# Two experts per token chosen tile by tile, with three of the choices inside later norms

## What is computed

```
u = rmsnorm(x) * (1 + sc1) + sh1
m = mixer(u)                       # input projection, RG-LRU group and retention group, output projection
x = x + g1 * rmsnorm(m)
u2 = rmsnorm(x) * (1 + sc2) + sh2
p_group = softmax(u2 @ w_rg + b_rg)                # 4 groups
g_sel = argmax(p_group)
e_logits = u2 @ w_re + b_re                        # 16 experts, 4 a group
top_w, top_i = top_k(softmax(e_logits of g_sel), 2)
f = sum of the two experts (256 wide, silu-gated), weighted by p_g * top_w / sum(top_w)
x = x + g2 * rmsnorm(f)
```

## Time and profile before

| | us |
|---|---|
| median of three runs | 573.47 (573.0 to 574.8) |
| the profiled execution, its own time | 574.29 |
| its span in the profile | 572.3 |
| TensorE busy | 550.2 (96% of the span) |
| DVE busy | 212.0 (37%) |
| ScalarE busy | 166.4 (29%) |
| POOL busy | 98.5 (17%) |
| mean granted clock of TensorE | 0.991 |

### The profile page before, as it was taken

One profiled execution on the slowest core, in us unless ns is written; L12 is line 12 of the kernel. 1 busy time (PEld: TensorE's weight loads), 2 busy tenths in 40 slices (PEclk: granted clock), 3 DMA queues, 4 the chain that ended last, 5 costly groups with the idle time before them and its releaser, 6 DMA issues.

```text
span 572.3 us, 6747 instructions
## 1 busy us (share of the span) xinstructions
PE 550.2 (96%) x2562; PEld 341.4 (60%) x2562; DVE 212.0 (37%) x526; ACT 166.4 (29%) x326; POOL 98.5 (17%) x116
## 2 busy tenths in 40 slices
PE   7899999999999999999999999799999999999984
PEld 6577755544454555574444455677777777777641
DVE  3434386421232233325433656422223223221137
ACT  7332676712123122322323343111112112111142
POOL 3016000133000000003100211313232422232110
PEclk8999999999999999999999999999999999999998
DMA  8999997899300000089400359969999999999564
GB/s 278 356 332 338 333 351 318 296 389 340 133 1 0 0 1 1 1 286 350 118 37 37 111 177 314 274 229 340 338 326 344 354 349 332 331 354 344 125 203 166
DMA packets 73492, 133.15 MB, mean 233 GB/s; under 512 B 4138, under 2 KB 49618, under 8 KB 71410
## 3 DMA queue, kind: packets, MB, share of 16 engines
q1 hardware_dynamic: 58864, 99.36, 50.3%
q0 software_dynamic: 9536, 28.75, 18.1%
q10 hardware_dynamic: 5058, 4.58, 2.4%
HBM read 117.47 MB, written 18.35 MB: 237 GB/s over the span
## 4 chain that ended last, share of the span: by engine, by line
PE 87%; DVE 5%; DMA 4%; ACT 2%; issue 1%; ACTq 0%; SPq 0%
PE psum L717 82%; PE psum L720 4%; DMA ring<-in_w_mod_dram 2%; DMA out_dram<-arena 1%; DVE arena L2203 1%; ACT arena L1365 1%; DVE x L2207 1%; DMA hy<-in_c_sample_dram 1%; DVE arena L2044 0%; ACT L1365 0%; DVE arena L2125 0%; DVE arena L2258 0%; ACT ss L1365 0%; ACTq L1605 0%; ACT hy L1365 0%
## 5 line engine op out<-in xcount | busy, mean ns | idle before, releaser
L717 PE MATMUL psum<-ring,arena 128*128 128x256 f32 (+1 forms) x640 | 173.5, 427 | 1.8 <-DVE arena L2258 1.3
L717 PEld LDWEIGHTS psum<-ring,arena 128*128 128x128 f32 x640 | 120.3, 192 | 38.8 <-issue 25.8
L717 PE MATMUL psum<-ring,uT 128*128 128x512 f32 (+1 forms) x384 | 126.5, 522 | 0.0
L1365 ACT ACTIVATE arena<-psum 128x512 f32<-128x512 f32 (+6 forms) x111 | 50.7, 478 | 229.8 <-PE psum L717 202.8
L717 PEld LDWEIGHTS psum<-ring,uT 128*128 128x128 f32 (+1 forms) x384 | 56.5, 172 | 60.1 <-issue 55.8
L717 PE MATMUL psum<-uT,ring 128*128 128x288 f32 x256 | 64.9, 410 | 1.3 <-ACT uT L1365 1.3
L717 PEld LDWEIGHTS psum<-uT,ring 128*128 128x128 f32 x256 | 47.7, 190 | 17.5 <-issue 5.1
L720 PEld LDWEIGHTS psum<-con,arena 128*128 128x128 f32 (+1 forms) x295 | 35.5, 145 | 21.4 <-issue 14.1
L720 PE MATMUL psum<-con,arena 128*128 128x128 f32 (+1 forms) x295 | 42.2, 280 | 4.1 <-DVE arena L2303 3.1
L2303 DVE TENSOR_TENSOR arena<-arena,psum 128x256 f32<-128x256 f32 x16 | 6.7, 421 | 98.5 <-ACT arena L1365 98.5
L1365 ACT ACT_TABLE_LOAD x33 | 42.3, 1283 | 3.1 <-issue 2.1
(11 more groups left out here) (214 smaller groups left out, 421.8 us busy)
## 6 DMA issues: line engine op xcount, KB each, us to landing
ring<-in_w_mod_dram SPq DMA_DIRECT2D x24, 1024.0 KB, 11.4
ring<-in_w_exp_gate_dram SPq DMA_DIRECT2D x16, 1024.0 KB, 10.9
ring<-in_w_exp_up_dram SPq DMA_DIRECT2D x16, 1024.0 KB, 16.6
ring<-in_w_exp_down_dram SPq DMA_DIRECT2D x16, 1024.0 KB, 11.7
ring<-in_w_in_dram SPq DMA_DIRECT2D x10, 1024.0 KB, 14.3
ring<-in_w_out_dram SPq DMA_DIRECT2D x4, 1024.0 KB, 14.9
f_dram<-in_consts_dram POOLq DMA_DIRECT2D x1, 3072.0 KB, 20.5
arena<-in_state_ret_dram POOLq DMA_DIRECT2D x6, 512.0 KB, 5.4
```

What stands on the lines that cost most here:

```text
L717: return nc.tensor.matmul(out, lhsT, rhs, start=first, stop=last)
L1365: return nc.scalar.activation(out, src, func, **kw).then_inc(done, 1)
```

## The change

Each tile's choice is made alone, by `first_choice(t)` and `second_choice(t)`, with per-partition scalars where the version before had broadcast tensors. Tile 0's is put into `after_mixer(2)`, tile 1's into `after_mixer(3)`, the first part of tile 2's into `after_mixer(4)`, all between the count of `s_x1` and the wait for the root; the second part of tile 2's comes behind `after_mixer(4)`, and those of tiles 3 and 4 behind their `take_logits`. `s_rsel` now counts tiles. The difference of logits for the gates and one comparison for all tiles follow behind the last choice. On TensorE, the sum of tile 3's logits comes ahead of tile 4's transposes, with two fillers ahead of it; the second half of `state_step(1)` moves behind the rank sums, `add_state(1)` behind the first `slot_tokens`, and the four fillers ahead of the wait for `sel` go. The buffers of the choice lie elsewhere in the same arena.

```diff
--- before.py
+++ after.py
@@ -267,8 +267,8 @@
         gx = rtb[:, 0:25].rearrange("p (t g) -> p t g", g=5)
         rtop, rtmp, rm1, rm2 = (rtb[:, 25 + 5 * i:30 + 5 * i] for i in range(4))
         rgrp = rtb[:, 48:68].rearrange("p (t g) -> p t g", g=NG)
-        lem = region(14336 + 2 * TILES * NE, TILES, NE)
-        oh = [region(14336 + i * TILES * NE, TILES, NE) for i in range(2)]
+        lem = region(12800 + 2 * TILES * NE, TILES, NE)
+        oh = [region(12800 + i * TILES * NE, TILES, NE) for i in range(2)]
         rank1 = region(14336 + 3 * TILES * NE, TILES, NE)
         gsl = [region(14784 + i * NE, NE) for i in range(2)]
         spare = region(14816, 1)
@@ -1174,19 +1174,19 @@
             pair_sum(1)
             state_step(0, (1,))
             route_parts(3)
+            keep_running(2, 1)
+            route_sum(3)
             turn_u2(4)
-            route_sum(3)
             keep_running(3, 1)
             route_parts(4)
             keep_running(1, 1)
             route_sum(4)
             add_state(0)
-            state_step(1)
+            state_step(1, (0,))
 
 
             pe.wait_ge(s_u2Te, 2 * TILES)
-            keep_running(4, 4)
-            pe.wait_ge(s_rsel, 1)
+            pe.wait_ge(s_rsel, TILES)
             pe.wait_ge(s_clear, 6)
             pe.wait_ge(s_x1, TILES)
             pe.wait_ge(s_lg, TILES)
@@ -1200,7 +1200,7 @@
                 last = mm(bank[7][:, TILES * NE:(TILES + 1) * NE], ones[0:n], sel[0:n, j], j == 0,
                           j == TILES - 1)
             last.then_inc(s_rank, 1)
-            add_state(1)
+            state_step(1, (1,))
 
             def slot_tokens(e):
 
@@ -1213,6 +1213,7 @@
                 last.then_inc(s_tokn, 1)
 
             slot_tokens(0)
+            add_state(1)
 
             with pe.If(fits(pe)):
                 def turn_input(e):
@@ -2058,6 +2059,42 @@
 
             tag = lambda t: "p" if t < TILES - 1 else "s"
 
+            def first_choice(t):
+
+                dve.wait_ge(s_lg, t + 1)
+                lg, le, one = logit[:, t, 0:NG], logit[:, t, NG:], slice(t, t + 1)
+                grp, code = rgrp[:, t], oh[0][:, t]
+                link(v.tensor_reduce(out=rtop[:, one], in_=lg, axis=AX.X, op=ALU.max))
+                link(v.scalar_tensor_tensor(out=grp, in0=lg, scalar=rtop[:, one],
+                                            in1=con[:, C_REV + NE - NG:C_REV + NE],
+                                            op0=ALU.is_equal, op1=ALU.mult))
+                link(v.tensor_reduce(out=rtmp[:, one], in_=grp, axis=AX.X, op=ALU.max))
+                link(v.tensor_scalar(grp, grp, rtmp[:, one], 3.0e38, ALU.is_equal, ALU.mult))
+                link(v.scalar_tensor_tensor(
+                    out=lem[:, t].rearrange("p (g e) -> p g e", e=EPG),
+                    in0=grp.unsqueeze(2).to_broadcast([P, NG, EPG]), scalar=-3.0e38,
+                    in1=le.rearrange("p (g e) -> p g e", e=EPG), op0=ALU.add, op1=ALU.add))
+                link(v.tensor_reduce(out=rm1[:, one], in_=lem[:, t], axis=AX.X, op=ALU.max))
+                link(v.scalar_tensor_tensor(out=code, in0=lem[:, t], scalar=rm1[:, one],
+                                            in1=con[:, C_REV:C_REV + NE], op0=ALU.is_equal,
+                                            op1=ALU.mult))
+                link(v.tensor_reduce(out=rtmp[:, one], in_=code, axis=AX.X, op=ALU.max))
+                link(v.tensor_scalar(code, code, rtmp[:, one], None, ALU.is_equal))
+
+            def second_choice(t):
+
+                one, code = slice(t, t + 1), oh[1][:, t]
+                link(v.scalar_tensor_tensor(out=lem[:, t], in0=oh[0][:, t], scalar=-3.0e38,
+                                            in1=lem[:, t], op0=ALU.mult, op1=ALU.add))
+                link(v.tensor_reduce(out=rm2[:, one], in_=lem[:, t], axis=AX.X, op=ALU.max))
+                link(v.scalar_tensor_tensor(out=code, in0=lem[:, t], scalar=rm2[:, one],
+                                            in1=con[:, C_REV:C_REV + NE], op0=ALU.is_equal,
+                                            op1=ALU.mult))
+                link(v.tensor_reduce(out=rtmp[:, one], in_=code, axis=AX.X, op=ALU.max))
+                v.scalar_tensor_tensor(out=sel[:, t], in0=code, scalar=rtmp[:, one],
+                                       in1=oh[0][:, t], op0=ALU.is_equal, op1=ALU.add)\
+                    .then_inc(s_rsel, 1)
+
             def after_mixer(t):
                 w = D if t < TILES - 1 else HALF
                 dve.wait_ge(s_mrms, t + 1)
@@ -2073,6 +2110,10 @@
                 link(last)
                 v.tensor_tensor(out=x[:, t, 0:w], in0=x[:, t, 0:w], in1=u2[t % 2][:, 0:w],
                                 op=ALU.add).then_inc(s_x1, 1)
+                if t >= 2:
+                    first_choice(t - 2)
+                if t in (2, 3):
+                    second_choice(t - 2)
                 dve.wait_ge(s_x1rms, t + 1)
                 link(v.reciprocal(ss[:, 2, t, 0:1], ss[:, 2, t, 0:1]))
                 if t >= 2:
@@ -2114,41 +2155,21 @@
             after_mixer(3)
             take_logits(2)
             after_mixer(4)
-            take_logits(3)
-            take_logits(4)
-
-
-            dve.wait_ge(s_lg, TILES)
-            lg, le = logit[:, :, 0:NG], logit[:, :, NG:]
+            second_choice(2)
+            for t in range(TILES - 2, TILES):
+                take_logits(t)
+                first_choice(t)
+                second_choice(t)
 
             def tt(out, a, b, op):
                 link(v.tensor_tensor(out=out, in0=a, in1=b, op=op))
 
-            def first_max(src, top, onehot, n):
-                shape = [P, TILES, n]
-                rev = con[:, C_REV + NE - n:C_REV + NE][:, None, :].to_broadcast(shape)
-                link(v.tensor_reduce(out=top, in_=src, axis=AX.X, op=ALU.max))
-                tt(onehot, src, top.unsqueeze(2).to_broadcast(shape), ALU.is_equal)
-                tt(onehot, onehot, rev, ALU.mult)
-                link(v.tensor_reduce(out=rtmp, in_=onehot, axis=AX.X, op=ALU.max))
-                tt(onehot, onehot, rtmp.unsqueeze(2).to_broadcast(shape), ALU.is_equal)
-
-            first_max(lg, rtop, rgrp, NG)
-            v.tensor_tensor(out=gx[:, :, 0:NG], in0=lg,
+            v.tensor_tensor(out=gx[:, :, 0:NG], in0=logit[:, :, 0:NG],
                             in1=rtop.unsqueeze(2).to_broadcast([P, TILES, NG]),
                             op=ALU.subtract).then_inc(s_gin, 1)
-
-            link(v.tensor_scalar(rgrp, rgrp, 3.0e38, -3.0e38, ALU.mult, ALU.add))
-            link(v.tensor_tensor(
-                out=lem.rearrange("p t (g e) -> p t g e", e=EPG),
-                in0=le.rearrange("p t (g e) -> p t g e", e=EPG),
-                in1=rgrp.unsqueeze(3).to_broadcast([P, TILES, NG, EPG]), op=ALU.add))
-            first_max(lem, rm1, oh[0], NE)
-            link(v.scalar_tensor_tensor(out=lem, in0=oh[0], scalar=-3.0e38, in1=lem, op0=ALU.mult,
-                                        op1=ALU.add))
-            first_max(lem, rm2, oh[1], NE)
-            v.tensor_tensor(out=sel[:], in0=oh[0], in1=oh[1], op=ALU.add).then_inc(s_rsel, 1)
             v.tensor_tensor(out=gx[:, :, 4], in0=rm2, in1=rm1, op=ALU.subtract).then_inc(s_gin, 1)
+            dve.wait_ge(s_rsel, TILES)
+            tt(oh[1], oh[1], rtmp.unsqueeze(2).to_broadcast([P, TILES, NE]), ALU.is_equal)
 
             def gate_weights():
                 dve.wait_ge(s_gexp, 2)
```

## The result

The changed kernel takes 580.01 us (median of 16 runs), the kernel before 575.51 in the same comparison: ratio 1.0067, with a 95% interval of 1.0043 to 1.0091. It is 0.67% slower, 3.9 us, clear of the 0.3% that a measurement can tell. The two medians lie 4.5 us apart, since one of the 16 runs, 585.31 us, is over 1.5% above the fastest and is left out of the ratio; without it the median is 579.33. The kernel before came out 2.0 us above the 573.47 that its first three runs had given, so the 576.9 that was forecast from that base is to be read as a distance too, +3.4 us or 1.0060.

The account below looks back on a forecast made before the run. TensorE's products were taken as 87% of the chain, so DVE counts only where TensorE stands still, as ahead of sel. DVE 1.6 + order 0.9 + clock 0.9 = +3.4 us on 573.47 gave 576.9 us, range 572.2 to 578.9.

Parts of the forecast that it names:

- the base: Whole kernel: starting time 573.47 us, the median of the kernel before, to which the forecast's +3.4 us was added.
- the clock: TensorE around sel: idle time and narrow work lower the granted clock, costing 0.9 us, bounds 0 and 1.7.
- the stores of u2: Ahead of the rank step: issued some 2 us later, landing around 349 to 350, costing nothing.
- DVE's high bound: DVE up to sel: 3.6 us for each choice and 0.75 from tile 2, summing to +3.2 us.
- A choice: One tile's choice on DVE: 14 small steps taking 3.1 us, bounds 2.8 and 3.6.
- Tile 2's norm: DVE in tile 2's norm: tile 0's choice overruns the idle time, so tile 3's norm starts 0.7 us later.
- DVE from x1 of tile 2 to `sel`: DVE's queue up to sel: choices overrun idle times, so sel is ready at 350.1, 1.6 us later.
- Order on TensorE: TensorE behind sel: moved work costs +0.9 us up to the first expert; third token sum at 8.3 us behind sel.
- The store wait absorbs nothing: Behind the first expert's start: the 7.15 us store wait shifts along with DVE's state steps and hides no delay.
- order cost only: Rival: steps near 2.8, no clock fall, sel about as before, +0.9 us from order, 574.4 us; chance 0.2.
- faster: Rival: choices of tiles 0 to 2 hidden, sel 1.8 us earlier; 572.6 us, or 570.9 without the later clock fall; chance 0.17.
- absorbed: Rival: ScalarE's wait for the state store ends on something else, so the shift vanishes, 573.5 us; chance 0.03.

Follow-up runs that it names:

- e4: Changed kernel without the choices of tiles 0 to 2, whose tokens go to no expert; ratio 1.0003 to the kernel before.
- e3: Changed kernel with seven TensorE fillers put back ahead of the wait for sel; ratio 1.0131 to the kernel before.
- e11: Changed kernel with ScalarE waiting only for the stores of states 0 and 1, plus seven fillers ahead of the wait for sel; ratio 1.0071 to the kernel before.
- e5: Kernel before with ScalarE waiting only for the stores of states 0 and 1 ahead of the first expert's activation; ratio 0.9925 to the kernel before.
- e2: Kernel before with only TensorE's order of the changed kernel and no fillers ahead of sel; ratio 1.0051 to the kernel before.
- e9: Changed kernel's choices with TensorE's order of before, and ScalarE waiting only for the stores of states 0 and 1; ratio 0.9992 to the kernel before.
- e6: Changed kernel with ScalarE waiting only for the stores of states 0 and 1; ratio 1.001 to the kernel before.
- e10: Kernel before with TensorE's order of the changed kernel, and ScalarE waiting only for the stores of states 0 and 1; ratio 0.9988 to the kernel before.
- e7: Kernel before with choices of tiles 0 to 2 cut into DVE's idle times, tiles 3 and 4 chosen together, two fillers; ratio 0.9999 to the kernel before.
- e1: Changed kernel with TensorE's order of before, so the choices alone; ratio 1.0079 to the kernel before.
- e12: Kernel before with choices cut into DVE's idle times, split state-store wait, and first hit list moved to unused arena; ratio 0.9952 to the kernel before.

## Why the prediction was right or wrong

The direction and the path were right: a late `sel` out of DVE's queue, work moved behind it on TensorE, a clock fall. The distance was near, +3.4 us forecast and +3.9 measured, and 1.0060 lies within the interval. The time itself, 580.01, lies 3.1 us above the 576.9 of the forecast and above the range's end of 578.9. The step that failed is the base, "the median of 573.47, to which I hold": it was the median of three runs of a kernel whose 16 runs spread from 573.0 to 578.1 with a median of 575.51. That is 2.0 of the 3.1 us, and the range took in the bounds of the terms but not of this; with 575.51 it would have reached 580.9. The other 1.1 us are terms that were mis-sized, the clock above all (0.9 forecast, some 2 by the clock time lost), and the stores of u2, put at nothing.

That 3.4 came so near to 3.9 is in part luck, and doesn't bear out the sizes of the terms: in the profile the stretch up to the first expert costs 4.4 us, with DVE, clock and stores above their terms and only the order below. By its own numbers DVE's high bound, with 3.6 us for a choice, adds up to +3.5 and not +3.2; the range would have ended at 579.2, still too low.

By its steps:
- **A choice**: 3.1 us forecast, 3.2 measured, with the extra 0.05 for a scalar from memory (0.22 and 0.23 against 0.16 and 0.17).
- **Tile 2's norm**: 0.7 forecast for tile 3's start. It was 1.35 (329.76 less 1.02, against 327.39), since a small step in the middle of the choice stood beside POOL for 3.46 us and the rest of the choice had to follow it.
- **DVE from x1 of tile 2 to `sel`**, with the two terms above in it: 1.6 forecast, 1.8 to 1.9 measured in every kernel with these choices (33.23 to 33.27 against 31.4). e4 shows that the choices of tiles 0 to 2 did it. The term is settled.
- **Order on TensorE**: 0.9 forecast. Where the clock held, the first expert came 11.88 (e3) and 11.59 us (e11) behind `sel` against 10.6: 1.0 to 1.3, with the next point in it. The rank step was 0.67 (e3) and 0.28 us (e11, against e5) later behind `sel`; without that the order itself is 0.6 to 0.7. The third sum of tokens, forecast at 8.3 us behind `sel`, stood at 8.7 and 8.5 there, and at 10.0 in the changed kernel.
- **The stores of u2**, costed at nothing with the words that they land around 349 to 350: the median of the two was 7.5 us instead of 6.7, the last took 8.40 and landed at 352.68, and DVE's rank step, 1.12 us behind `sel` before, came at 1.35 after and at 1.79 in e3. So 0.2 to 0.7. This was another step that failed, a cover with too little left. How much of it is the change's is open: e2 and e5, whose choice is the one of before, waited for the same store until 1.60 and 1.22.
- **The branch** on DVE took 1.36 us where it took 0.99, not foreseen. It cost nothing in the changed kernel, where the hit list behind it was done at 357.10 and TensorE took it at 359.47; in e9, with TensorE's order of before, TensorE took it at 355.14, right behind its end at 355.09, and this is the 0.24 us there.
- **Clock**: 0.9 forecast, with 1.7 as the bound. In the changed kernel's profile, 13.14 less the 11.6 to 11.9 of the kernels with full clock: 1.3 to 1.5. In e6 it was 2.5 to 2.8, beyond the bound, since the low level lasted 6 us, where the fall of the kernel before lasted some 3.5 (371 to 375). Averaged over executions 7.8 us were lost against 5.4 to 6.2, and 6.2 in e6 against 4.0 in e5. The term was mis-sized by about a factor of two.
- **The store wait absorbs nothing**: right; it grew by 0.7 in this profile.

The rivals: "order cost only" is refuted by `sel`; "faster" fell at the point that was named, the gap of 1.54 us in tile 3's norm; "absorbed" (the time of before) is refuted by the ratio, and e6 against e5 has the loss without the store wait too.

The Trainium skill's sentence on small tiles (VectorE: DVE Perf Modes, section on the TRN2 errata) is borne out: 14 steps on up to 16 columns take 3.2 us, 19 on up to 80 columns 4.9. With the rule that the default is throttled and activity releases it (the Trainium skill, TensorE: Matmul & The Clock Gate, section on the HAM clock gate) the traces agree too: in the five profiles where TensorE was idle 1.4 to 2.5 us ahead of `sel` (the changed kernel, e2, e4, e6, e10) the granted clock fell behind it, and in the other nine, idle 0.23 to 0.67 us there, it did not. But such idle time doesn't make the fall sure, as the prediction took it from that rule. Behind the first expert TensorE in e7 had the same work and nearly the same idle times as the kernel before in the earlier trace rows (2.21 and 0.36 us):

```profile
368.96 0.44 PE L720 MATMUL psum<-con,arena 128*128 128x128 f32 x2 [2.12 <-DVE arena L2356]
369.76 7.14 PE L717 MATMUL psum<-ring,arena 128*128 128x256 f32 x32 [0.36 <-DVE arena L2311]
```

and the granted clock stayed at 1.00, with the 32 products in 7.14 us and not 8.83.

What stays open: why the fillers of e3 and e11 cost 3 to 4 us in time while their profiles are better up to the first expert, and with it what the clock fall behind `sel` is worth in the average execution, since no run took it away and got the time back; how e1's 4.5 us divide beyond the 2.6 of its profile; and whether choices that keep clear of POOL's work in tile 2's norm would gain.

## What to carry to other kernels

Cutting a batched chain of small vector steps into one chain per tile multiplies the work; it pays only where every piece fits, in whole, into an idle time that was there before, and the first place where it doesn't (here 3.2 us into 1.54) pushes everything behind it. Count what else a pulled-ahead result needs before it can be used (here stores that landed 8.4 us after issue), or the gain moves into that wait. Work of TensorE ahead of a wait has its share in the clock behind it: where it was moved away and the wait stayed (e2, e10), the clock fell. Putting fillers back is no sure cure (e3, e11); judge it by the runs and not by one profile.

## What was not expected of the hardware

- DVE's branch took 0.99 us in the kernels with one choice for all tiles and in e4 (before, e2, e4, e5, e10), and 1.36 in those with more instructions ahead of it (changed, e1, e3, e6 to e9, e11, e12). The cause is open.
- One and the same pair of idle times, 2.1 to 2.2 and 0.36 us around two transposes, was followed by a fall of the granted clock in the kernel before and e2, and by none in e7.
- Executions of one kernel differ mostly by the clock: over the 16 runs of the changed kernel, time and mean granted clock go against each other with a correlation of -0.92, from 575.96 us at 0.991 to 585.31 at 0.978.
- A step of 16 columns on DVE (its like 0.23) took 3.46 us beside POOL's issue of two transfers (1.76 us) and product (1.91), and ended 0.03 behind that product; the product of 1024 columns had taken 3.76 there (its like 1.28). A reduction of 16 columns just ahead, which began at 319.65 beside the same issue, took its usual 0.17.
